# Hybrid attention block on one core: values as the stationary operand, probabilities normalised before the turn, turned copies on ScalarE, one row maximum per pair of groups

## What is computed

```python
h = rmsnorm(x, g_mix)
qa, ka, va, cq, ckv, kr, gate_a, gate_b = split(h @ w_in)
sc = q @ k.T * scale                      # per head and chunk of 128 queries
p = softmax(where(kpos <= qpos, sc, -inf))
o = p @ v                                 # (queries, 64) per head
y = sigmoid(gate_a + b0) * (o_a @ w_o_a) + sigmoid(gate_b + b1) * (o_b @ w_o_b)
x = x + y @ w_out
u = relu(rmsnorm(x, g_mlp) @ w_ff1)
x = x + (u * u) @ w_ff2
return rmsnorm(x, g_final)
```

## Time and profile before

| | us |
|---|---|
| time, median of 3 runs | 387.92 |
| lowest and highest | 387.61 and 387.93 |
| the profiled execution's own time | 388.31 |
| its span, first to last instruction | 386.1 |
| busy in the span: PE, DVE, ACT | 374.4, 230.5, 189.8 |
| mean granted clock of TensorE | 0.996 of full speed |

### The profile page before, as it was taken

The page is one execution under the profiler, slowest core; times in us unless marked ns, Lnnn a source line. Parts: engine busy times, 40 slices in busy tenths (PEclk is TensorE's granted clock), DMA queues, the critical chain, the costliest instruction groups (busy, mean ns, idle before and its releaser), DMA issues.

```text
span 386.1 us, 5653 instructions
## 1 busy us (share of the span) xinstructions
PE 374.4 (97%) x2222; PEld 330.9 (86%) x2222; DVE 230.5 (60%) x293; ACT 189.8 (49%) x315; POOL 16.6 (4%) x39
## 2 busy tenths in 40 slices
PE   6999999999999999999999999999999999999992
PEld 6998889877888888888899898998989899898982
DVE  0976973926656766669387665474455537445325
ACT  4995426955455445145265555254435525443313
POOL 4211000000000100000120000000000000000002
PEclk9999999999999999999999999999999999999998
DMA  7998667643322355409354684656465564630002
GB/s 239 340 388 266 235 192 244 219 161 111 111 105 109 132 196 169 159 2 303 132 165 164 232 312 149 218 178 217 131 202 210 161 216 166 217 109 0 1 2 109
DMA packets 38722, 67.29 MB, mean 174 GB/s; under 512 B 2305, under 2 KB 21505, under 8 KB 38449
## 3 DMA queue, kind: packets, MB, share of 16 engines
q1 hardware_dynamic: 36800, 63.44, 48.9%
q0 software_dynamic: 720, 3.35, 2.4%
q10 hardware_dynamic: 1184, 0.27, 0.3%
HBM read 66.00 MB, written 1.05 MB: 174 GB/s over the span
## 4 chain that ended last, share of the span: by engine, by line
PE 92%; DVE 3%; ACT 2%; DMA 2%; issue 1%; POOL 0%; SPq 0%; ACTq 0%; DVEq 0%; POOLq 0%
PE ps L1002 28%; PE ps L1004 27%; PE ps L1003 27%; PE ps L1009 4%; PE ps L1150 3%; PE ps L1123 2%; DMA xs<-in_x_dram 2%; DVE wlo L678 1%; DVE negmax L788 1%; ACT prob L535 1%; ACT whi L398 0%; PE ps L1114 0%; ACT xT_hi L398 0%; DVE prob L797 0%; DVE xT_lo L742 0%
## 5 line engine op out<-in xcount | busy, mean ns | idle before, releaser
L398 ACT ACTIVATE whi<-raw 128x1024 fp32r<-128x1024 f32 (+3 forms) x124 | 120.7, 1011 | 56.9 <-PE ps L1004 55.6
L678 DVE TENSOR_TENSOR wlo<-raw,whi 128x1024 fp32r<-128x1024 f32 (+3 forms) x74 | 80.9, 1127 | 25.2 <-ACT whi L398 25.2
L924 DVE TENSOR_TENSOR wlo<-raw,whi 128x1024 fp32r<-128x1024 f32 x50 | 60.0, 1222 | 34.0 <-ACT whi L398 34.0
L1002 PE MATMUL ps<-whi,xT_hi 128*128 128x512 f32 (+3 forms) x208 | 79.0, 380 | 0.7 <-DVE wlo L678 0.4
L1004 PE MATMUL ps<-whi,xT_lo 128*128 128x512 f32 (+3 forms) x208 | 75.6, 363 | 0.0
L1003 PE MATMUL ps<-wlo,xT_hi 128*128 128x512 f32 (+3 forms) x208 | 75.3, 362 | 0.0
L1002 PE MATMUL ps<-whi,lat_hi 128*128 128x512 f32 (+1 forms) x180 | 70.0, 389 | 0.0
L1003 PE MATMUL ps<-wlo,lat_hi 128*128 128x512 f32 (+1 forms) x180 | 69.5, 386 | 0.0
L1004 PE MATMUL ps<-whi,lat_lo 128*128 128x512 f32 (+1 forms) x180 | 69.5, 386 | 0.0
L1004 PE MATMUL ps<-xT_hi,wlo 128*128 128x256 f32 x224 | 63.4, 283 | 0.0
L1003 PE MATMUL ps<-xT_lo,whi 128*128 128x256 f32 x224 | 63.4, 283 | 0.0
(11 more groups left out here) (96 smaller groups left out, 292.9 us busy)
## 6 DMA issues: line engine op xcount, KB each, us to landing
raw<-in_w_ff_dram SPq DMA_DIRECT2D x32, 1024.0 KB, 5.2
raw<-in_w_in_dram SPq DMA_DIRECT2D x14, 1024.0 KB, 5.8
raw<-in_w_out_dram SPq DMA_DIRECT2D x4, 1024.0 KB, 5.0
gates<-in_b_gate_dram POOLq DMA_DIRECT2D x2, 1024.0 KB, 7.8
raw<-in_w_o_a_dram SPq DMA_DIRECT2D x2, 1024.0 KB, 4.9
raw<-in_w_o_b_dram SPq DMA_DIRECT2D x2, 1024.0 KB, 5.0
raw<-in_w_in_dram SPq DMA_DIRECT2D x2, 576.0 KB, 10.6
raw<-in_w_q_up_dram SPq DMA_DIRECT2D x2, 576.0 KB, 4.9
```

The lines of the kernel that those rows point to most:

```text
L398: return nc.scalar.activation(dst, src, ACT.Copy, scale=scale)
L678: nc.vector.tensor_tensor(wlo[:, s, h * w:(h + 1) * w], raw[:, s, h * w:(h + 1) * w], whi[:, s, h * w:(h + 1) * w].bitcast(F32), ALU.subtr ...
L924: nc.vector.tensor_tensor(wlo[:, s, h * w:(h + 1) * w], raw[:, s, h * w:(h + 1) * w], whi[:, s, h * w:(h + 1) * w].bitcast(F32), ALU.subtr ...
L1002: nc.tensor.matmul(dst, a_hi, b_hi, start=start, stop=False)
```

## The change

The value product has its operands exchanged: the 64 value columns of a head are stationary and the 128 turned probabilities move, so that the output comes out already turned, head by head on partitions 0 to 63 or 64 to 127 of bank 7 (`O_BANK`), in the order in which `oT_hi` and `oT_lo` want it. `turn_o` and `o_norm` fall away. Since the output no longer has queries on partitions, the probabilities are divided by their sums before they are turned (`p_scale`, DVE, once per group, in place). The copy of the turned probabilities goes to ACT. DVE takes the row maxima of two groups in one instruction. `oT_high` and `oT_low` come a step earlier (`O_STEP` is 4, 8, 10, 14), and in both engines' programs the weight's split comes ahead of the attention's part.

```diff
-O_STEP = [g + G_SLOT + 3 for g in O_GROUP]
+O_STEP = [g + G_SLOT + 2 for g in O_GROUP]
+O_BANK = 7
...
@@ ScalarE
-                act.wait_ge(max_ready, g + 1)
+                act.wait_ge(max_ready, g // 2 + 1)
...
-                act.wait_ge(o_turned, j + 1)
+                act.wait_ge(pv_done, O_GROUP[j] + 1)
...
+            def pT_copy(g):
+                act.wait_ge(p_turned, g + 1)
+                if g >= 2:
+                    act.wait_ge(pv_done, g - 1)
+                copy(prob[:, 2 + g % 2, :], ps[:, 6, :]).then_inc(pT_ready, 1)
...
-                if 0 <= s - G_SLOT < NG:
-                    exps(s - G_SLOT)
                 high(U_GATE + AHEAD + s // 2, s % 2)
                 if s % 4 == 3 and s > 3:
                     tanh_rows(s // 4 - 1)
+                if 0 <= s - G_SLOT < NG:
+                    exps(s - G_SLOT)
+                if 0 <= s - G_SLOT - 1 < NG:
+                    pT_copy(s - G_SLOT - 1)
...
@@ VectorE
+            def row_max(pair):
+                heads = GROUPS[2 * pair][2]
+                n = len(heads)
+                top = negmax[:, 2 * pair:2 * pair + 2, 0:n]
+                dve.wait_ge(scored, pair + 1)
+                nc.vector.tensor_reduce(top.rearrange("p g (j b) -> p b (g j)", b=2) if n == 4 else
+                                        top.rearrange("p g b -> p b g"),
+                                        ps[:, S_BANK:S_BANK + 2, :].rearrange("p b (j k) -> p b j k", j=n),
+                                        AX_X, ALU.max, negate=True).then_inc(max_ready, 1)
+
+            def p_scale(g):
+
...
+                keys, n = P * (t + 1), len(heads)
+                r = rrow[:, 2 * path + t, heads[0]:heads[0] + n]
+                dve.wait_ge(p_ready, g + 1)
+                nc.vector.reciprocal(r, rowsum[:, 2 * path + t, heads[0]:heads[0] + n]).then_inc(rrow_ready, 1)
+                dve.wait_ge(rrow_ready, g + 1)
+                p = prob[:, g % 2, :].rearrange("p (h k) -> p h k", h=n)
+                nc.vector.tensor_tensor(p, p, r.unsqueeze(2).broadcast_to([P, n, keys]),
+                                        ALU.mult).then_inc(p_scaled, 1)
...
+                if s % 4 == 0 and s > 0:
+                    if s == 4:
                         dve.wait_ge(bias_landed, 32)
                     gate_rows(s // 4 - 1)
+                low(U_GATE + AHEAD + s // 2, s % 2)
+                if 0 <= s - G_SLOT < NG:
+                    if (s - G_SLOT) % 2 == 0:
+                        row_max((s - G_SLOT) // 2)
+                    p_scale(s - G_SLOT)
...
@@ TensorE
             def turn_p(g):
-                pe.wait_ge(p_ready, g + 1)
+                pe.wait_ge(p_scaled, g + 1)
...
-                for i, h in enumerate(heads):
+                for i in range(0, len(heads), 2):
                     for kb in range(t + 1):
-                        b = i * (t + 1) + kb
-                        m = nc.tensor.matmul(ps[:, 7, h * 64:(h + 1) * 64], prob[:, 2 + g % 2, b * P:(b + 1) * P],
-                                             v[:, kb, h * 64:(h + 1) * 64], start=(kb == 0), stop=(kb == t))
+                        for j in (i, i + 1):
+                            h, b = heads[j], j * (t + 1) + kb
+                            m = nc.tensor.matmul(ps[h % 2 * 64:h % 2 * 64 + 64, O_BANK, h // 2 * P:(h // 2 + 1) * P],
+                                                 v[:, kb, h * 64:(h + 1) * 64],
+                                                 prob[:, 2 + g % 2, b * P:(b + 1) * P],
+                                                 start=(kb == 0), stop=(kb == t))
                 m.then_inc(pv_done, 1)
-
-            def turn_o(j):
-                pe.wait_ge(o_rows, j + 1)
-                pe.wait_ge(pT_ready, min(O_GROUP[j] + 2, NG))
-                turn(6, blocks(rows[:, j, :]), P, o_turned)
```

More of the change, by code:

```diff
@@ L197, in hybrid_block @@
         rrow_ready = sem("rrow_ready")
-        o_rows = sem("o_rows")
-        o_turned = sem("o_turned")
+        p_scaled = sem("p_scaled")
         oT_hi_done = sem("oT_hi_done")
@@ L550, in oT_high @@
                 path, t = divmod(j, 2)
-                act.wait_ge(o_turned, j + 1)
+                act.wait_ge(pv_done, O_GROUP[j] + 1)
                 copy(oT_hi[:, path, :, t * P:(t + 1) * P],
-                     ps[:, 6, :].rearrange("p (b s) -> p b s", b=4)).then_inc(oT_hi_done, 1)
+                     ps[:, O_BANK, :].rearrange("p (b s) -> p b s", b=4)).then_inc(oT_hi_done, 1)
+            def pT_copy(g):
[3 more added lines that the diff above has]
+                copy(prob[:, 2 + g % 2, :], ps[:, 6, :]).then_inc(pT_ready, 1)
             for s in range(STEPS):
@@ L782, in _ @@
             low_unit(16)
-            def row_max(g):
-                path, t, heads = GROUPS[g]
[L786 to L809, removed]
+            def row_max(pair):
[7 more added lines that the diff above has]
+                                        AX_X, ALU.max, negate=True).then_inc(max_ready, 1)
@@ L814, in oT_low @@
                 nc.vector.tensor_tensor(oT_lo[:, path, :, t * P:(t + 1) * P],
-                                        ps[:, 6, :].rearrange("p (b s) -> p b s", b=4),
+                                        ps[:, O_BANK, :].rearrange("p (b s) -> p b s", b=4),
                                         oT_hi[:, path, :, t * P:(t + 1) * P].bitcast(F32),
@@ L1132, in turn_p @@
                     pe.wait_ge(pT_ready, g)
-                if g - 2 in O_GROUP:
-                    pe.wait_ge(oT_lo_done, O_GROUP.index(g - 2) + 1)
                 turn(6, blocks(prob[:, g % 2, :]), P, p_turned)
@@ L1144, in values @@
                 if g - 1 in O_GROUP:
-                    pe.wait_ge(o_rows, O_GROUP.index(g - 1) + 1)
+                    pe.wait_ge(oT_lo_done, O_GROUP.index(g - 1) + 1)
                 v = (v_a, v_b)[path]
-                for i, h in enumerate(heads):
+                for i in range(0, len(heads), 2):
                     for kb in range(t + 1):
-                        b = i * (t + 1) + kb
-                        m = nc.tensor.matmul(ps[:, 7, h * 64:(h + 1) * 64], prob[:, 2 + g % 2, b * P:(b + 1) * P],
-                                             v[:, kb, h * 64:(h + 1) * 64], start=(kb == 0), stop=(kb == t))
+                        for j in (i, i + 1):
[4 more added lines that the diff above has]
+                                                 start=(kb == 0), stop=(kb == t))
                 m.then_inc(pv_done, 1)
-            def turn_o(j):
-                pe.wait_ge(o_rows, j + 1)
-                pe.wait_ge(pT_ready, min(O_GROUP[j] + 2, NG))
-                turn(6, blocks(rows[:, j, :]), P, o_turned)
             for s in range(STEPS):
@@ L1176, in _ @@
                     values(s - G_SLOT - 1)
-                if s + 1 in O_STEP:
-                    turn_o(O_STEP.index(s + 1))
             def mixer_out(i):
```

## The result

The changed kernel takes 384.74 us (median of 4 runs, 384.22 to 385.16) against 387.93 beside it; the ratio is 0.9917, 95% interval 0.9905 to 0.9929. It is faster by 3.2 us, 0.8%. The forecast was 386.5: the right way, but 1.4 us of gain where 3.2 came.

The account below looks back on a forecast made before the run. PE was taken as the bound, busy 374.4 of 386.1 us. Terms -1.8 - 0.6 + 0 + 1.05 = -1.35 from the median 387.92 gave 386.55, stated as 386.5; own range 385.1 to 387.8, wide range 383.0 to 389.1.

Parts of the forecast that it names:

- Turns: Four sets of four output transposes vanish from PE, 0.44 us each: 1.8 us less.
- Value blocks: The 12 blocks of eight value matmuls on PE fall from 0.90 to 0.85 us each: 0.6 us less.
- with the same toll: Value blocks pay 0.40 us for entering and leaving the divided array, as the scores do: 0.45 + 0.40 = 0.85.
- Rival 1: Value blocks: the column halves pair up without a toll, gaining 5.4 instead of 0.6 us; 382.2 us; chance 0.14.
- rival 2: Value blocks: no pairing and no toll, blocks stay at 0.90 us; 387.2 us; chance 0.12.
- Rival 3: Value blocks cost more than before: 389.1 us with loads in sequence, 392.0 with no pairing; decides from 0.96 upward; chance 0.16.
- Group 0: Stage's start: the 1.0 us wait before values(0) goes, one of the same size replaces it (0.8 before the turn): sum 0.
- New waits: PE waits before values: 0.1 at steps 4 and 10 together, 0.5 at step 8, 0.15 at 7, 0.3 at 5: +1.05 us.
- Rival 4: The change's waits on PE are twice those worked out: +1.05 us, 387.6 us; chance 0.12.
- Moves at no cost: Earlier gates, weight splits up to 1.5 us later on DVE, and POOL's two loads cost PE nothing.

Follow-up runs that it names:

- Experiment 5: Changed kernel with four idle transposes put back at each of the four places where the output's turns stood: 386.36 us, ratio 0.9962 to the kernel before.
- experiments 3 and 4: Changed kernel plus one idle whole-array matmul per value block: in its middle (3) 388.27 us, at its end as control (4) 384.68 us.
- experiment 2: Changed kernel with every value matmul in the lower half of the array's columns, one head after the other: 389.97 us, ratio 1.0047 to the kernel before.
- experiment 1: Changed kernel with value matmuls issued so that neighbours go to the same half of the array's columns: 384.79 us, ratio 0.9916 to the kernel before.
- experiment 11: Changed kernel without reciprocal and scaling, the turn waiting for the exponentials alone: 384.67 us, ratio 0.9909 to the kernel before.
- Experiment 9: Changed kernel with the first pair's maximum in two halves and the copy ahead of the exponentials at steps 2 and 7: 383.93 us, ratio 0.9894.
- experiment 6: Changed kernel with row maxima as before, one 512-column instruction per group at its own step: 398.78 us, ratio 1.0265 to the kernel before.
- experiment 8: Changed kernel with the copy of the turned probabilities back on VectorE, last in its step: 395.13 us, ratio 1.0185 to the kernel before.

## Why the prediction was right or wrong

Its sum was -1.35 and the stage gained 3.41. By its terms:

- **Turns, -1.8: right.** Experiment 5 gives 1.6 by its time and 1.9 by its profile, the removed set of step 4 to 5 is 0.44.
- **Value blocks, -0.6: the mechanism right, the size wrong.** A block in front of a product gains 0.11 (step 6, 4.11 to 4.00), one in front of the mask 0.14 (98.16 to 104.14 less the turn's 0.44 is 5.54, 98.00 to 103.40 is 5.40). Seven and five of them make 1.5. The step that failed is "with the same toll": 0.40 was taken from the scores' way in and out, and measured by experiments 3 and 4 the value blocks' toll is 0.30. With it my own sum would have been 0.45 + 0.30 = 0.75, 12 x 0.15 = 1.8, now a little too much: step 6 shows 0.79 (0.69 read as in the prediction, 103.40 to 104.32 less 0.23, and 0.10 more on the way in). The pairing, on which all else hung, is shown by experiment 2 and the starts. Rival 1 (no toll) is refuted by experiment 3, rival 2 (no pairing) by experiment 2.
- **Why the old block was beatable.** I set 0.90 against 8 x 0.11 and didn't ask why a pass of 64 columns should take as long as one of 128. Its first two starts, 0.055 apart, show that such a pass can take half of that; something else set the 0.11, the load of 128 columns as I suppose, which no run tested.
- **Rival 3, slower.** Its point of decision, a block of 0.96, was not reached: loads and passes do overlap between halves that share their rows. At step 6 the eight loads and eight passes all start within 0.39 us, and even in one half (experiment 2), with a load ahead of every pass, the passes start 0.11 apart, which is a pass's own length. The Trainium skill's rule (TensorE: Matmul & The Clock Gate, Part 3), that loads overlap a matmul in flight only for another row group, is contradicted here. What the Trainium skill says there on the order of matmuls, strictly that of the program, doesn't fit either with experiments 1 and 2 taken together. The Trainium skill's statement in TensorEngine Tiling, Key Properties, that a change of mode drains the array agrees with the 0.30.
- **Group 0, 0: right**, 5.81 and 5.84. Why was only half seen: I gave the wait to maximum and scaling, and experiment 11 shows a second chain of the same length on ACT. Experiment 9 shortens both, and gains 0.4.
- **New waits, +1.05: too high, 0.4.** They are those of steps 7 and 8, 0.2 each; step 8 is the one that I had at 0.5. PE reaches the values at 113.72, and then (changed kernel, ACT and PE alone):

```profile
113.72 0.66 PE L1150 MATMUL ps<-prob,v_a 128*64 128x128 f32 x8
...
114.43 0.60 ACT L398 ACTIVATE lat_hi<-ps 128x512 fp32r<-128x512 f32 x1 [0.76 <-PE ps L1150]
...
114.92 1.05 ACT L398 ACTIVATE whi<-raw 128x1024 fp32r<-128x1024 f32 x1
...
115.87 0.36 ACT L535 ACTIVATE prob<-ps,negmax 128x128 f32<-128x128 f32 x1
...
117.24 0.62 ACT L398 ACTIVATE prob<-ps 128x512 f32<-128x512 f32 x1
...
117.91 0.66 PE L1150 MATMUL ps<-prob,v_b 128*64 128x128 f32 x8
```

  The chain was the one foretold: split, rounding, four exponentials, copy. But from start to start they take 0.49, 0.95, 1.37 and 0.67, 3.5 where I had 0.6 + 1.0 + 1.4 + 0.6 and 0.1 for the handover. Step 8 takes 4.19, 0.2 above step 6, where I had 0.5. Two thirds of the difference are that I had priced split and rounding by durations, which overlap with the next start; the rest is that PE's own work from one block to the next is 3.3 (4.00 - 0.69) and not 3.2, by the longer way in. Step 5, by the same error on DVE, doesn't wait at all (5.40, shorter than before): its maximum starts 0.3 behind the scores, not 0.6. Step 7 waits 0.2 (foretold 0.15). Steps 4 and 10 are 4.00.
- **Missing: an old wait.** Before, values(8) started 0.2 late behind the copy (4.33 from values(7), against 4.11); the changed kernel takes 4.00 there. The list of waits doesn't hold it, and I read only the list. Besides, the two old blocks behind a wait, values(0) and values(8), had their first two starts 0.16 apart instead of 0.055 and so took 0.1 more each. Together that is 0.4 that could be gained.
- **Rival 4, the waits doubled:** they were well under half of what I had. **Moves at no cost:** right; no wait for a weight is listed for PE in the stage.

The measured terms are -1.8, -1.5, -0.4 and +0.4, -3.3 of the 3.41; the last 0.1 to 0.2 I can't place. The three errors, 0.9 at the blocks, 0.7 at the new waits and 0.4 at the old ones, all had the same sign, which is why the time fell outside the forecast's own range (385.1 to 387.8) while within the wide one. That own range was also added up wrongly at its upper end: by its own bounds of the waits and the block it would reach 388.1.

## What to carry to other kernels

A product with a small output width is worth turning round where both halves of the array can be filled: here a block of eight passes fell from 0.90 to between 0.76 and 0.79 us, toll included, and sets of transposes went with it. Longer blocks should gain more, by an estimate from these rows: two further passes take 0.11 us as a pair instead of 0.22, and the toll of 0.3 us is paid once per block. Price the pieces of a busy engine's queue from start to start, not by durations. And before an instruction on the second engine is split or moved, ask which group's result is early because of it: the pair's maximum, twice as long, saves 14 us over two short ones at the wrong place, lower clock included.

## What the runs showed of the hardware

- An idle bf16 matmul of 128x128 behind a value block costs PE nothing measurable (384.68 against 384.74 us; the step is 4.03 against 4.00).
- Leaving and entering the array divided by columns costs 0.30 us together (experiments 3 and 4: 3.6 us for twelve).
- TensorE pairs passes of the two column halves although the program issues one half's four first (experiment 1: starts in pairs 13 ns apart, 8 passes within 0.67 us; in one half 1.09 and single starts 0.11 apart).
- A block of full width with 64 moving columns has its first two starts 0.055 us apart when it follows without a wait, and 0.16 behind a wait (values(0) and values(8) of the kernel before); the further starts are 0.11 apart in either case.
- With waits of up to 3.1 us before the values (experiment 6) the granted clock over the stage fell from 1.00 to 0.92. In experiment 8 it fell behind the wait of 1.9 us at step 4 (0.72 over 100 to 106) and not behind one as long at step 8 (1.00 over 110 to 130).
